# Retention in a new order: the next head's v product between scores and P·V, and v turned by VectorE blocks and small transfers

## The reference

```
proj = h @ w_in
q, k, v, g = jnp.split(proj, [D_MODEL, 2 * D_MODEL, 4 * D_MODEL], axis=-1)
q, k = rotary(q, pos), rotary(k, pos) * RET_QK_DIM ** -0.5
o[n] = sum over m of (q[n] . k[m]) * gamma_h ** |n - m| * v[m]      # both directions together
y = silu(g) * (o - mean(o)) * rsqrt(var(o) + RMS_EPS)               # mean and var over a head's 512
return y @ w_out
```

## Time and profile before

| what | value |
|---|---|
| median of 3 runs | 713.92 us (713.9 to 714.15) |
| profiled execution | 713.68 us, of which span 711.9 us |
| TensorE matmul | 702.4 us busy, 99% of the span |
| VectorE, ScalarE, GpSimd | 606.9, 519.7, 27.3 us busy |
| granted TensorE clock | 1.0 of full speed |
| retention | heads 0 to 3 end at 47.8, 88.9, 130.0 and 171.1 us |

### The profile page before, as it was taken

One profiled execution on the slowest core, in us unless ns is written; L12 is line 12 of the kernel. 1 busy time (PEld: TensorE's weight loads), 2 busy tenths in 40 slices (PEclk: granted clock), 3 DMA queues, 4 the chain that ended last, 5 costly groups with the idle time before them and its releaser, 6 DMA issues.

```text
span 711.9 us, 15944 instructions
## 1 busy us (share of the span) xinstructions
PE 702.4 (99%) x6540; PEld 589.5 (83%) x6540; DVE 606.9 (85%) x819; ACT 519.7 (73%) x850; POOL 27.3 (4%) x28
## 2 busy tenths in 40 slices
PE   8999999999999999999999999999999999999996
PEld 6888887878899888888888998888888888885464
DVE  6969877777889799989898879999999999999643
ACT  7566674857576688778788677899768888987431
POOL 0010010101010000000001400000000000000000
PEclk9999999999999999999999999999999999999999
DMA  9763363453572356555579961110535665666821
GB/s 347 290 232 126 112 237 119 173 183 113 205 285 111 103 197 232 185 182 215 186 277 381 349 238 61 60 60 1 197 105 204 209 218 203 225 226 208 263 42 59
DMA packets 28634, 132.07 MB, mean 186 GB/s; under 512 B 11040, under 2 KB 11552, under 8 KB 13344
## 3 DMA queue, kind: packets, MB, share of 16 engines
q1 hardware_dynamic: 28288, 130.96, 51.3%
q10 hardware_dynamic: 288, 0.31, 0.1%
HBM read 129.17 MB, written 1.05 MB: 183 GB/s over the span
## 4 chain that ended last, share of the span: by engine, by line
PE 91%; DVE 3%; ACT 3%; DMA 1%; issue 1%; SPq 0%; DVEq 0%
PE ps L1609 23%; PE ps L1610 23%; PE ps L1611 23%; PE ps L2038 3%; PE ps L2040 3%; PE ps L2039 3%; PE ps L1652 2%; PE ps L1656 2%; PE ps L1651 2%; PE ps L1731 1%; PE ps L1728 1%; PE ps L1727 1%; PE ps L1978 1%; DMA stage<-in_chunks 1%; PE ps L1858 1%
## 5 line engine op out<-in xcount | busy, mean ns | idle before, releaser
L1609 PE MATMUL ps<-a_hi,w_hi 128*128 128x272 f16 (+1 forms) x1000 | 276.9, 277 | 0.0
L1611 PE MATMUL ps<-a_hi,w_lo 128*128 128x272 f16 (+1 forms) x1000 | 276.9, 277 | 0.0
L1610 PE MATMUL ps<-a_lo,w_hi 128*128 128x272 f16 (+1 forms) x1000 | 276.9, 277 | 0.0
L990 DVE SCALAR_TENSOR_TENSOR w_lo<-stage,w_hi 128x1024 f16<-128x1024 f32 x207 | 246.4, 1222 | 34.7 <-ACT w_hi L525 34.3
L525 ACT ACTIVATE w_hi<-stage 128x1024 f16<-128x1024 f32 x207 | 208.7, 1044 | 28.1 <-PE ps L2040 18.3
L1609 PEld LDWEIGHTS ps<-a_hi,w_hi 128*128 128x128 f16 x1000 | 97.8, 98 | 16.9 <-DVE rs L999 0.9
L1611 PEld LDWEIGHTS ps<-a_hi,w_lo 128*128 128x128 f16 x1000 | 97.8, 98 | 15.9
L1610 PEld LDWEIGHTS ps<-a_lo,w_hi 128*128 128x128 f16 x1000 | 97.8, 98 | 15.8
L1609 PE MATMUL ps<-y_hi,w_hi 128*128 128x272 f16 (+3 forms) x496 | 106.1, 242 | 0.0
L1610 PE MATMUL ps<-y_lo,w_hi 128*128 128x272 f16 (+3 forms) x496 | 106.1, 242 | 0.0
L1611 PE MATMUL ps<-y_hi,w_lo 128*128 128x272 f16 (+3 forms) x496 | 106.0, 242 | 0.0
(11 more groups left out here) (277 smaller groups left out, 1096.9 us busy)
## 6 DMA issues: line engine op xcount, KB each, us to landing
stage<-in_chunks SPq DMA_DIRECT2D x118, 1024.0 KB
stage<-in_chunks SPq DMA_DIRECT2D x3, 512.0 KB
decay_all<-in_decay SPq DMA_DIRECT2D x1, 1056.0 KB, 13.2
work<-work SPq DMA_DIRECT2D x32, 32.0 KB, 2.0
out<-sq SPq DMA_DIRECT2D x4, 256.0 KB, 2.1
hT<-in_tokens SPq DMA_DIRECT2D x3, 272.0 KB, 6.1
stage<-in_chunks SPq DMA_DIRECT2D x2, 256.0 KB
mT<-in_gains SPq DMA_DIRECT2D x1, 512.0 KB, 7.7
```

Source lines behind the costliest of these rows:

```text
L990: dve.scalar_tensor_tensor(out=part(1, c, q), in0=flat(stage, c, q), scalar=W_SCALE, in1=part(0, c, q), op0=ALU.mult, op1=ALU.subtract).th ...
L1609: pe.matmul(o, w_h, x_h, start=start, stop=False)
L1610: pe.matmul(o, w_h, x_l, start=False, stop=False)
L1611: return pe.matmul(o, w_l, x_h, start=False, stop=stop)
```

## The change

The v chunk becomes the first of a head (`c`), q/k the second (`c + 1`), g the third. TensorE's order from scores on is now: scores of head h, v chunk of head h+1, P·V of head h, then q/k and gate of head h+1. After the last head's scores the first half of `RET_OUT` stands in place of the next v. The heads alternate their two sets of banks (`HEAD_BANKS`), and the next v chunk goes into the banks of the gate, so it waits for `g_out`. v is no longer transposed by TensorE: VectorE turns 32x32 blocks straight out of PSUM (`v_evict`), SyncE moves the blocks into place by 20 transfers per head (`load_v_rows`), and ScalarE applies the token's scale there, for which `rs_in` itself is turned once by three transposes and read into `rs_tok`. `parameters()` and `lru_rates()` now stand ahead of the rotation of heads 0 and 1.

```diff
-        STAT_IN = [Y + 3, X + 3, Y + 3, Y + 3]
+        STAT_IN = [X + 3, X + 3, Y + 3, Y + 3]
+        HEAD_BANKS = [(X, Y), (Y, X), (X, Y), (Y, X)]
 
 
...

+            def load_v_rows(h):
+
+                sp.wait_ge(v_out, h + 1)
+                from_blocks = v_blocks.rearrange("p e (n m) -> p (e n) m", m=P)
+                for f in range(4):
+                    for r in range(4):
+                        rows, cols = slice(32 * r, 32 * (r + 1)), slice(32 * f, 32 * (f + 1))
+                        sp.dma_start(v_rows[rows, :, cols], from_blocks[cols, :, rows]).then_inc(v_landed, 16)
+                for f in range(4):
+                    sp.dma_start(v_last[0:META, :, 32 * f:32 * (f + 1)],
+                                 v_edge[32 * (f + 1) - META:32 * (f + 1), :, :]).then_inc(v_landed, 16)
+
             for c in range(1, FFN0_IN):
                 load(c)
+                if c in [RET_IN[h] + 3 for h in range(HEADS)]:
+                    load_v_rows(c // 3 - 1)
...
+            def head_out(h):
+
+                bank = HEAD_BANKS[h][0]
+                act.wait_ge(o_up, h + 1)
+                if h:
+                    act.wait_ge(ylo_made, h)
+                for n in range(4):
+                    act.activation(oT[:, n, :], ps[:, bank + n, 0:T], ACTF.Copy, scale=1.0 / A_SCALE ** 2)
+                for n in range(4):
+                    last = act.activation(osq[:, n, :], ps[:, bank + n, 0:T], ACTF.Square, scale=1.0 / A_SCALE ** 2)
+                last.then_inc(o_sq, 1)
...
+                for q in range(3):
+                    prep(c + 2, q)
                 if h:
+                    head_out(h - 1)
+                prep(c + 2, 3)
+                for q in range(3):
+                    prep(c + 3, q)
+                if h:
                     act.wait_ge(s_up, h)
+                qk_high(0)
+                qk_high(1)
+                prep(c + 3, 3)
+
+                if h == 0:
+                    act.wait_ge(rst_made, 1)
+                act.wait_ge(v_landed, 20 * 16 * (h + 1))
+                for n, (_, m) in enumerate(TOK_TILES):
+                    act.activation(vs[n][0:m], vs[n][0:m], ACTF.Identity, scale=rs_tok[0:m, n:n + 1],
+                                   accum_out=vsum[0:m, n, 0:1]).then_inc(vs_out, 1)
...
+                prep(c + 4, 0)
...
+                act.wait_ge(g_out, h + 1)
+                act.activation(gT, gT, ACTF.Silu, scale=-0.5 * UNSCALE).then_inc(g_silu, 1)
                 if h:
                     head_y(h - 1)
                 for q in range(1, SUB):
...
+            head_out(HEADS - 1)
...
+            def v_evict(h):
+
+                bank = HEAD_BANKS[h][0] if h else Y
+                dve.wait_ge(w_used, used(RET_IN[h]))
+                dve.transpose(v_blocks, ps[:, bank:bank + 4, 0:2 * P])
+                dve.transpose(v_edge, ps[:, bank:bank + 4, T - 32:T]).then_inc(v_out, 1)
+
+            def head_gated(h):
+
+                dve.wait_ge(g_silu, h + 1)
+                dve.wait_ge(o_sq, h + 1)
+                mark(dve.scalar_tensor_tensor(out=oT, in0=oT, scalar=-A_SCALE / 2, in1=gT, op0=ALU.mult,
+                                              op1=ALU.mult))
...
+                for q in range(3):
+                    prep(c + 2, q)
+                if h:
+                    head_gated(h - 1)
+                    gated_at[h - 1] = step[0]
+                prep(c + 2, 3)
+                for q in range(3):
+                    prep(c + 3, q)
+                if h == 0:
+                    parameters()
+                    dve.wait_ge(rst_up, 1)
+                    for n, (_, m) in enumerate(TOK_TILES):
+                        last = dve.tensor_scalar(rs_tok[0:m, n:n + 1], ps[0:m, Y + 3, n * P:n * P + 1],
+                                                 -0.5 * UNSCALE * A_SCALE, None, ALU.mult)
+                    last.then_inc(rst_made, 1)
+                elif h == 1:
+                    lru_rates()
+
...
+                dve.wait_ge(w_used, used(c + 1))
                 for x, op in ((0, ALU.subtract), (1, ALU.add)):
                     mark(dve.tensor_tensor(rot[:, x], qk[:, x], cos, ALU.mult))
                     link(dve.tensor_tensor(rotp[:, x], qk[:, 1 - x], sin, ALU.mult))
                     dve.tensor_tensor(rot[:, x], rot[:, x], rotp[:, x], op).then_inc(rot_done, 1)
...
+                qk_low(0)
+                qk_low(1)
+                prep(c + 3, 3)
...
-                prep(c + 3, 0)
+                prep(c + 4, 0)
+
+                dve.wait_ge(w_used, used(c + 2))
+                times_rs(gT, G).then_inc(g_out, 1)
+                dve.wait_ge(s_up, h + 1)
+                for n, (m0, m) in enumerate(TOK_TILES):
+                    last = dve.tensor_tensor(sT[0:m, n, :], ps[0:m, A + n, 0:T],
+                                             decay_sb[0:m, h, 2 * P - m0:2 * P - m0 + T], ALU.mult)
+                last.then_inc(s_dec, 1)
+                if h:
+                    rsqrt(rs, A + 3, 0, ESTIMATE[("head", h - 1)])
+                dve.wait_ge(shi_made, h + 1)
                 if h:
                     head_y(h - 1)
-                    parameters()
-                    prep(c + 3, 1)
-
-                dve.wait_ge(w_used, used(c + 2))
-                times_rs(gT, X).then_inc(g_out, 1)
+                prep(c + 4, 1)
+                prep(c + 4, 2)
                 if h:
                     head_low(h - 1)
-                    prep(c + 3, 1)
-                prep(c + 3, 2)
-                prep(c + 3, 3)
-                for q in range(SUB):
-                    prep(c + 4, q)
-                if h == 0:
-                    lru_rates()
-
+                prep(c + 4, 3)
+                if h + 1 < HEADS:
+                    v_evict(h + 1)
+            head_gated(HEADS - 1)
+            gated_at[HEADS - 1] = step[0]
...
+                A, G = HEAD_BANKS[h]
                 if h:
-                    pe.wait_ge(g_out, h)
-                    chunk(c, X, a_hi, a_lo, 0, 0)
+                    pe.wait_ge(v_out, h + 1)
+                    chunk(c + 1, A, a_hi, a_lo, 0, 0)
                     pe.wait_ge(o_sq, h)
-                    chunk(c + 1, Y, a_hi, a_lo, 0, 0)
+                    chunk(c + 2, G, a_hi, a_lo, 0, 0)
                 else:
-                    chunk_first()
-                    chunk_bank3_last(c + 1, Y, a_hi, a_lo, 0, mean_input(0, 0), 0, stat_in_read(0))
+                    chunk_bank3_last(c + 1, A, a_hi, a_lo, 0, mean_input(0, 0), 0, stat_in_read(0))
+                    pe.wait_ge(v_out, 1)
+                    pe.wait_ge(ident_landed, 16)
+                    for n, (m0, m) in enumerate(TOK_TILES):
+                        mm = pe.transpose(ps[0:m, Y + 3, n * P:(n + 1) * P], rs_in[:, m0:m0 + m], ident_sb[:])
+                    mm.then_inc(rst_up, 1)
+                    chunk(c + 2, G, a_hi, a_lo, 0, 0, bank3=lambda: pe.wait_ge(rst_made, 1))
                 pe.wait_ge(rot_done, 2 * h + 2)
                 if h:
-                    head_norm(h - 1, GN)
+                    head_norm(h - 1, A + 3)
-                pe.wait_ge(v_out, h + 1)
-                if h == 0:
-                    pe.wait_ge(ident_landed, 16)
-                for n, (m0, m) in enumerate(TOK_TILES):
-                    for e in range(4):
-                        mm = pe.transpose(ps[0:m, Y + n, e * P:(e + 1) * P], vT[:, e, m0:m0 + m], ident_sb[:])
-                mm.then_inc(vt_up, 1)
-                pe.wait_ge(s_dec, h + 1)
-                chunk(c + 2, X, a_hi, a_lo, 0, 0, bank3=head_norm_read(h - 1) if h else None)
-
-                pe.wait_ge(vs_out, NTT * (h + 1))
+                pe.wait_ge(g_out, h + 1)
+                if h + 1 < HEADS:
+                    chunk(RET_IN[h + 1], G, a_hi, a_lo, 0, 0)
+                else:
+                    chunk(RET_OUT, X, y_hi, y_lo, 0, 0, last=False, need=heads, ks=range(KC // 2))
+
                 pe.wait_ge(vlo_made, h + 1)
                 for e in range(4):
+                    if h and e == 3:
+                        pe.wait_ge(rs_made, ESTIMATE[("head", h - 1)])
...
-            pe.wait_ge(g_out, HEADS)
-            chunk(c, X, y_hi, y_lo, 0, 0, last=False, need=heads, stat=lambda: head_norm(HEADS - 1, Y),
-                  stat_k=6)
-            chunk(c + 1, X, y_hi, y_lo, KC, 0, first=False, need=heads)
+            chunk(c, X, y_hi, y_lo, 0, 0, last=False, need=heads, ks=range(KC // 2, KC))
+            chunk(c + 1, X, y_hi, y_lo, KC, 0, first=False, need=heads, stat=lambda: head_norm(HEADS - 1, Y), stat_k=0)
```

More of the change, by code:

```diff
@@ L206, in build @@
         rotq = carve(4, T)
-        vs = carve(3, BANK)
+        v_blocks = carve(4, 2 * P)
+        v_edge = carve(4, 32)
+        v_rows = carve(8, P)
+        v_last = carve(4, P)
+        vs = [v_rows.rearrange("p (e n) m -> p n e m", n=2)[:, n] for n in range(2)] + [v_last]
+        rs_tok = sb("rs_tok", [P, NTT])
         sT = rotq[:, 0:3, :]
         oT, gT = mT[:, 0:4, :], mT[:, 4:8, :]
```

(29 more changed lines are left out.)

119 lines of the change are left out of this document (33 added, 86 removed).

## The result

The changed kernel takes 722.95 us (median of four runs, 722.6 to 725.6) where the kernel before takes 713.91; the ratio is 1.0135, with a 95% interval from 1.0111 to 1.0159 (the ratio is that of the means; the medians differ by 9.04 us, 1.27%). The profiled execution took 722.61 us. The forecast was 717.8 with a range up to 722.0: the direction was right, and the size was less than half of what came (3.9 of 9.0 us).

A forecast was written before the change was run, and what follows sets the result against it. TensorE, whose matmuls fill 99% of the span, was taken to bound the kernel. Terms of -5.98 + 0.35 + 3.25 + 1.5 + 3.25 + 0.4 + 1.3 = +4.1 us on 713.68 gave 717.8 us, range 714.5 to 722.

The forecast's parts named there:

- the seven quarters of weights in head 0: VectorE's weight quarters before the `rs_tok` reads: 1.15 us each, 8.05 us, waiting for nothing else as ScalarE is idle.
- the 4.68 us from ScalarE's read-out to the sums in the tail: Last head: ScalarE's first read of P·V to the end of GpSimd's sums takes 4.68 us, by the earlier trace.
- What is removed, -5.98 + 0.35: TensorE, all heads: 48 transposes (5.44 us) and three scale waits (0.54) go; three transposes of `rs_in` add 0.35.
- The wait for the turned scale, 3.25: Head 0, fourth bank of the gate chunk: TensorE waits 3.25 us for VectorE's reads into `rs_tok`.
- The gate's waits: TensorE's next v chunk waits for `g_out`: 1.5 us in head 0, 3.25 in head 1, 0.2 each in heads 2 and 3.
- The tail, 1.3: After the last scores: TensorE's waits for head 3's sums and its `y_lo` cost a net 1.3 us.
- The wait for the sums: Tail: TensorE wants head 3's sums 14.4 us after `g_out`, they come at 15.6, a wait of 1.2 us.
- rival C: Clock falls to 1.2 GHz behind the two 3.25 us stalls, 1.7 to 3.5 us each: 720 to 724 us; chance 0.09.
- last `y_lo`: Tail: the chain to head 3's `y_lo` misses by 0.3 us, where 0.2 was lost before.
- B: Block transfers late, landing 5.8 us after issue or issued 0.8 apart: head 0 waits 2 to 4 us more, 719.8 to 722.5; chance 0.10.
- D: Faster: the chain from rotation to gate eviction overlaps more, gate waits and the tail's 1.2 us vanish: 711.4 us; chance 0.10.
- E: No change: head 1's rates or head 0's reads cost about half: 712.5 to 715.1 us; chance 0.07.

The follow-up runs named there:

- experiment 10: On top of experiment 9, gate of heads 1 to 3 evicted before v's low parts, head 2's v turned two quarters earlier: 711.13 us, ratio 0.996.
- experiment 8: Changed kernel with the 16 large block transfers of v made one plain transfer of the same 512 KB, blocks not placed: 723.17 us, ratio 1.0137.
- experiment 2: Changed kernel with `lru_rates()` cut in two halves, run behind `head_y` in heads 1 and 2: 719.4 us, ratio 1.0078.
- experiment 4: Changed kernel with unread filler matmuls on TensorE, 38 ahead of head 0's `rst_made` wait, 18 ahead of the last head's sums: 722.29 us, ratio 1.0113.
- experiments 6: Changed kernel, head 0 requeued: `rs_tok` read earlier, parameters behind the low scores, gate evicted early, head 1's v turned earlier: 718.99 us, ratio 1.0074.
- experiment 9: Changed kernel with the edits of experiments 2, 6 and 7 together: 712.07 us, ratio 0.9978; its six executions lie between 710.66 and 714.77 us.
- experiments 3: Changed kernel with the three reads of `rs_tok` moved behind `prep(c + 3, 0)` in head 0: 725.31 us, ratio 1.016.
- experiment 7: Changed kernel; in head 3, head 2's `y_lo` made ahead of weight quarters, VectorE's last gated product waits for GpSimd's sums: 719.98 us, ratio 1.0089.

## Why the prediction was right in direction and short in size

Three steps failed. The largest is a missing term: the sum takes every stall at its length and puts the clock behind it at nothing, where the runs show 3.9 us of slow matmuls. The second is the premise that the seven quarters of weights in head 0 "are not waiting for anything else": they waited for their data, and the wait was 4.6 us, not 3.25. The third is the 4.68 us from ScalarE's read-out to the sums in the tail, which were 5.6. The rest of the mechanism, VectorE's queue, held.

**What is removed, -5.98 + 0.35.** Right: 5.4 us by experiment 10, against 5.6, and 1.54 us in a head of it, as said.

**The wait for the turned scale, 3.25.** The mechanism was right, the size was not: the distance is 35.74 - 30.99 - 0.12 = 4.6 us. (TensorE's arrival at the fourth bank was put at 31.05, where its terms add up to 30.96; it came at 31.1.) The step that failed is "The seven quarters are not waiting for anything else: their high parts are made by an idle ScalarE from 22 us on". ScalarE was idle, but for lack of data: it waited for each half chunk, as its timeline above shows. In the kernel before, ScalarE comes to the same quarters only behind the rotation:

```profile
19.04 1.05 ACT L525 ACTIVATE w_hi<-stage 128x1024 f16<-128x1024 f32 x1
...
26.41 1.04 ACT L525 ACTIVATE w_hi<-stage 128x1024 f16<-128x1024 f32 x1
```

No row there shows when they land, and the absence of a wait was read as early data. But the trace of the kernel before had the rate of the transfers. Its stretch from 10 to 26 us, then that of the changed kernel:

```profile
10.00:26.00 16.00, 16.00 (x137) 13.42 (x135) 15.26 (x22) 8.97 (x14) 0.00 (x0) 1.00 1.03 422
```

```profile
10.00:26.00 16.00, 16.00 (x136) 13.43 (x135) 15.30 (x21) 10.79 (x15) 0.00 (x0) 1.00 1.02 422
```

At 422 GB/s 1 MB takes 2.5 us, an estimate that the landings bear out, and VectorE was placed at 2.3 us for the two quarters in it. The read of `rs_tok` came 1.5 us late: 0.9 is VectorE's wait for the seventh quarter, 0.4 its pace over the six before (1.22 us each, not 1.15), 0.2 the start. The transfers of v did not set this pace, which stood before the first of them was issued (25.33 us); their pieces have a share of some 0.6 us in the last landing (experiment 8).

**The gate's waits.** Head 1: 3.25 said, 3.4 by the distance from 89.85 to 93.35; experiment 2 shows the cause. The passes over v took 0.71 us by ScalarE's timeline, where 0.72 was taken. Heads 2 and 3: 0.2 each, as said. Head 0: 1.5 said, none seen, as the slow matmuls delayed TensorE past it; with these filled it came back as 1.87 us in experiment 4. That 1.5 us of the sum did not fall due is luck, and it hid part of the clock's cost.

**The tail, 1.3.** The wait for the sums was 2.3 us, not 1.2. ScalarE's read-out began 183.87 - 172.90 = 11.0 us after the half of `RET_OUT`, where 10.9 was placed; the step that failed is the 4.68 us from there to the sums, taken from the earlier trace rows, where VectorE's product did not run beside them. Now it is 189.48 - 183.87 = 5.6, and the second sum alone has grown by 0.93.

**The clock, rival C.** It held 0.09 of the chance and was the largest missing term: 2.2 us in head 0 and 1.7 in the tail. The argument against it, clock 1.0 in all slices, was no evidence, since that kernel has no wait over 1.1 us. The 3.5 us that it took for a slow stretch came from no row; the runs show 13 to 21 matmuls at 0.227 us, 3.0 to 4.8 us, at a cost of 1.4 to 2.3. Against the forecast the terms differ by 1.4 (scale) + 3.9 (clock) - 1.5 (gate, head 0) + 0.1 (gate, head 1) + 1.1 (sums) - 0.3 (last `y_lo`, no longer waited for) = 4.7 us: 717.8 + 4.7 = 722.5, and the profiled execution took 722.61. This closes the account of one trace; it is no test of its terms, which the experiments are.

**The other rivals.** B did not come, but more narrowly than the medians over all heads (0.61 us to issue one, 2.0 to land) let it seem. In head 0 the sixteen large ones were issued 0.75 us apart, where the forecast had 0.67 and B 0.8, and landed 3.1 us after issue in the median; the last of the twenty was issued at 39.30 and, with the 1.8 us of its kind, was there at about 41.1, not 39.9. ScalarE came to v at 41.27 and waited for none only because it was late itself. When experiments 6, 9 and 10 brought it forward, it waited 0.5, 1.8 and 1.0 us for them. D and E did not come.

## What to carry to other kernels

Where TensorE is full, an engine that must answer in time is judged by its queue, not by its busy share: list what stands between the answer and its inputs, and then who stands behind it, since moving one instruction forward hands the stall to the next. A stall costs its length and, in 17 of the 22 here from 1.96 us on, another 1.4 to 2.3 us of slow matmuls; add that to each one in the sum. A row of an engine that comes late to its data says nothing about when the data landed.

## What the hardware showed that was not expected

The clock fell behind waits as short as 1.96 and 2.17 us, and did not fall behind one of 3.22 us in the very same place where it fell behind as long a one in three other kernels (experiments 3, 4 and 8). Length alone does not decide, and executions of one kernel differ (experiment 9). What does decide is not shown here. The Trainium skill ("TensorE: Matmul & The Clock Gate", section "Why this matters for your kernels") says to avoid idle gaps between bursts of matmuls; these runs agree: no slow matmuls stand behind the four waits of up to 1.20 us, and the shortest wait with some behind it is 1.96 us.

VectorE's product of two operands in SBUF and GpSimd's sum delay each other: 2.46 and 1.69 us together, 1.29 and 0.76 us apart (experiment 7, and the earlier trace rows for the sum before). The Trainium skill ("SBUF — State Buffer", section "SBUF: two separate sides") says that such a pair takes turns, each holding a shared port for its whole instruction; the numbers fit that, as each was longer by about the length of one instruction of the other (1.2 beside 1.34, 0.93 beside 1.29).

VectorE's block transpose out of PSUM takes 1.25 us for 128x1024, the same as out of SBUF.
